# Where five modulation blocks and one feature transposition stand in two attention loops of a float32 two-block network

## The chip, the cores and the metric

The kernel runs on one core of a Trainium2 chip. The metric is the device time of one execution in microseconds (us); three runs of the kernel before gave 1543.00, 1543.26 and 1543.37 us, with a median of 1543.26 us.

## The reference, cut to what matters

The reference runs two networks one after the other over 256 tokens of width 1024, in float32. The change lies in layer 0 of the second network, in its mixer of two attentions. The input has 256 tokens of `x` and 256 tokens of `ctx`; a modulation vector, computed from `w_mod`, scales and shifts the normed input.

```python
mod_x = (s_x @ w_mod[l] + b_mod[l])[:, None, :]       # 6 x 1024 values, and the same for ctx
h_x = modulate(rms_norm(x, norm_g[l, 0]), sh1_x, sc1_x)
...
# even_mixer: grouped-query attention A (8 heads), then pairwise (differential) attention B (4 pairs)
o_a = map_query_blocks(lambda q: gqa_attend(q, ka_all, va_all), qa_x)
s = jnp.einsum('bqhjd,bshjd->bhjqs', q, k); p = softmax(s)          # B: two score maps per head pair
a = (p[:, :, 0] - lam * p[:, :, 1]); o_b = einsum('bhqs,bshe->bqhe', a, v)
o_b = (rms_norm(o_b, subln_g) * (1 - lam0))
out_x = jnp.concatenate([o_a, o_b], axis=-1) @ w_out
```

## The kernel before, in words

Every engine has its own instruction stream, written out by hand in the same order of work, and the streams meet at semaphores. `did(...)` raises the semaphore of an engine under a label, and `after(label)` is the value that another engine waits for. Float32 matrices are split into a high part (ScalarE, L1180) and a low part (VectorE, L1196), and each product is three matmuls (L601 to L603). All weights come in one stream of 1 MB chunks through SyncE's queue into three slots `raw` (L565). A chunk's DMA starts when the chunk three places before it in the stream has been used: a split weight chunk by VectorE's low part, a modulation chunk by TensorE itself, which reads it unsplit.

**PSUM banks.** TensorE takes a bank for each result with `job(label)`: the banks of a ring in turn, and it waits until the last result of that bank has been read. In both attentions of layer 0 the ring has seven banks, so that a job waits for the reader of the job seven places before it. The eighth bank, number 7, is taken by `side=2` alone. In the first attention it holds the two query blocks that `query_block` computes, in the second the first four products of the output projection (`product_block`).

**The first attention (`items_second(0, 0)`, kind A).** 32 items, each a head and a tile of 128 tokens: the first 16 with 256 keys, the others with 512. The loop `attend` runs over steps `i`. On TensorE a step does, in this order: the scores of items i and i+1, in even steps (L784); what `side_steps_halves` places there (turns of queries and keys, L1051; one eighth of a projection of queries, `query`, three matmuls); a modulation block if `mods_at` gives one; the transposes of the probabilities of item i-3 (L818); and the values of item i-4 (L846). A modulation block (`mod`, L732) is 16 matmuls over two raw chunks, and ahead of it come the four transposes of the modulation block before it (`turn_mod`, L716). ScalarE does per step: the copy of item i-3's transposed probabilities (L1369), the exponentials of item i (L1350), and then a turned query or key (L1617). VectorE does: the maxima of item i (L2032), the outputs of item i-5 (L2103). It copies a modulation row (L1945) in the step after TensorE's, ahead of the maxima in an even step and behind them in an odd one. Five blocks stand in this loop, in steps 3, 8, 13, 18 and 23. GpSimd computes the roots that scale queries and keys before they are turned (L2698, L2700).

**The second attention (kind B).** 16 items, each a head pair on a tile of 128 tokens: the first 8 with 256 keys, the others with 512. In step i TensorE does the two scores of item i (L784), side work, the transposes of item i-2 (L818) and the values of item i-3 (L846). The side work is two value projections (steps 1 and 3), the four turns `fo` of the mixed output into features (L687; steps 5, 6, 16 and 17), each read by ScalarE (L1244) and then by VectorE (L1811), and four products (steps 8 to 11). ScalarE: copy of item i-2's probabilities, two exponentials of item i, high part of a feature. VectorE: two maxima of item i (L2032), the combination of the two maps of item i-1 (L2077 to L2080), the outputs of item i-4 (L2098), and the low part of a feature, if one stands in the step.

The change touches `side_steps_pairs`, `side_steps_halves`, `mods_at`, `turn_feature` and `turn_mixed`.

Of the kernel before, what the change touches and what calls it, by code (L numbers as in the profile page):

```python
# [237 lines left out]
class Counts:  # L238
# [6 lines left out]
    def did(self, sem, *labels):  # L245

        n = self.now[sem] = self.now.get(sem, 0) + 1
        for label in labels:
            assert label not in self.marks, label
            self.marks[label] = (sem, n)  # L250
        return self.sems[sem], 1
# [8 lines left out]
    def after(self, *label):  # L260

        if self.known is None:
            return self.sems["tensor"], 1
        sem, n = self.known.marks[label]
        return self.sems[sem], n
# [15 lines left out]
def build(nc, T, out, counts):  # L281
    did, after = counts.did, counts.after
    with ExitStack() as ctx:
# [5 lines left out]
        def tile(stack, name, shape, dt=F32):  # L289
            return stack.enter_context(nc.sbuf_tensor(name, shape, dt))  # L290
# [73 lines left out]
        mix = tile(ctx, "mix", [P, 4, D])  # L364
# [113 lines left out]
        def side_steps_pairs():  # L478


            return ([(1, ("v2", 0, 1, 0)), (3, ("v2", 0, 1, 1))] + [(at, ("fo", j)) for j, at in enumerate((5, 6, 16, 17))]
                    + [(8 + k, ("product", k)) for k in range(4)]
                    + [(18 + n, ("weights", PLACE[UNIT["out2", 0, 1].w0] + n)) for n in range(2)])

# [16 lines left out]
        def side_steps_halves():  # L501

            return ([(0, ("keys", 0)), (1, ("keys", 1)), (4, ("roots",)),
                     (2, ("ahead", PLACE[UNIT["q2", 0, 1].w0] + 1)),
                     (9, ("turn", "q", 0)), (10, ("turn", "k", 0)), (11, ("turn", "q", 1)), (12, ("turn", "k", 1))]
                    + [(at, ("query", 2, k)) for k, at in enumerate((4, 5, 6, 7, 9, 10, 11, 12))]
                    + [(at, ("query", 3, k)) for k, at in enumerate((15, 16, 17, 19, 20, 21, 22, 24))]
                    + [(13, ("queries", 2)), (25, ("queries", 3))])

        def items_second(l, part):  # L510
# [8 lines left out]

        def mods_at(i, items, mods):  # L520

            n, beside = divmod(i - 3, 5)
            return [mods[n]] if beside == 0 and 0 <= n < len(mods) else []

        def item_info(it):

# [53 lines left out]
        def _(pe):  # L580
# [5 lines left out]
            def job(*label, side=0):  # L586

                banks = (state["banks"], (6, 7), (7,))[side]
                b = banks[turn[side] % len(banks)]
                turn[side] += 1  # L590
                if b in last:
                    pe.wait_ge(*after("read", *last[b]))
                last[b] = label
                counts.banks[label] = b
                return ps[:, b, :]
# [78 lines left out]
                    ins = mm(o[:, 0:rhs.shape[-1]], lhs, rhs, start=True, stop=True)  # L674
                ins.then_inc(*did("tensor", ("read", "spin", label)))

            def turn_feature(name, src, tiles, ready, j):

                o = job(name, j)
                if j == 0:  # L680
                    for r in ready:
                        pe.wait_ge(*after(*r))
                for q in range(2):
                    for i, t in enumerate(tiles):
                        k = 2 * j + q
                        c = (2 * q + i) * P
                        ins = nc.tensor.transpose(o[:, c:c + P], src(t)[:, k * P:k * P + P], ident[:, :])  # L687
                ins.then_inc(*did("tensor", (name, j)))

            def turn_features(name, src, tiles, ready):  # L690

                for j in range(4):
                    turn_feature(name, src, tiles, ready, j)

            def turn_mixed(l, g, j):

                tiles = (2 * g, 2 * g + 1)
                ready = []
                if j == 0:
                    ready = [("mixed out" if l else "first half out", l, t) for t in tiles]  # L700
                elif l == 0 and j == 2:
                    ready = [("mixed out", l, t) for t in tiles]
                for r in ready:
                    pe.wait_ge(*after(*r))
                turn_feature(("fo", l, g), lambda t: mix[:, t, :], tiles, [], j)

            pending = []

# [161 lines left out]
            def attend(items, mods, steps=()):  # L870

                lag = turned_behind(items)
                for i in range(len(items) + lag + 1):
# [38 lines left out]
                    for m in mods_at(i, items, mods):  # L912
                        mod(*m)
# [128 lines left out]
            for l in range(2):  # L1042
# [12 lines left out]
                for part in range(2 - l):  # L1055
# [32 lines left out]
                    beside = l == 1  # L1088
# [4 lines left out]
                    else:  # L1093
                        oldest = [state["banks"][(turn[0] + n) % 8] for n in range(8)]
                        state["banks"], turn[0] = [b for b in oldest if b != 7], 0
                    attend(items_second(l, part), mods_second(l, part),
                           side_steps_last() if beside else side_steps_pairs() if part else side_steps_halves())
                    if l == 0:
                        oldest = [state["banks"][(turn[0] + n) % 7] for n in range(7)]
# [3 lines left out]
                if l == 0:  # L1103
                    for n in range(2):
                        by_token(UNIT["out2", 0, n], ("out2", 0, n), (2, 3), feat=None if n else ("fo", 0, 1), last=False,
                                 half_made=() if n else (2,))
                        if n == 0:
                            for j in range(4):
                                turn_mixed(0, 0, j)
# [4 lines left out]
                    for g in (1, 0):  # L1114
                        for j in range(2):
                            for e in range(4):
                                if (g, j, e) == (1, 1, 2):
                                    turn_normed(0, 1, 0)
                                by_feature(UNIT["in", 0, j], ("in", 0, j, g), g * S, g * S + S, feat=None if j else ("n2", 0, g),
                                           tiles=[e], first=g == 1, last=g == 0)  # L1120
# [15 lines left out]
                for j in range(4):  # L1136
                    turn_mixed(1, 0, j)
# [83 lines left out]
        def _(act):  # L1221
# [381 lines left out]
            for l in range(2):  # L1603
# [41 lines left out]
                for part in range(2 - l):  # L1645
# [45 lines left out]
                    if l == 1:  # L1691
                        act.wait_ge(loads["odd"], 48)
                        save_gates(1)
                    attend(items, side_steps_last() if l else side_steps_pairs() if part else side_steps_halves())
                for t in range(nt):
                    act.wait_ge(*after("mixed out", l, t))
# [90 lines left out]
        def _(dve):  # L1787
# [341 lines left out]
            def attend(items, mods, steps=()):  # L2129
                for i in range(len(items) + 5):  # L2130
                    if i % 2 == 0:
                        for m in mods_at(i - 1, items, mods):
                            mod_row(*m)
                    if i < len(items):
                        maxima(i, items[i])
                    if i % 2:
                        for m in mods_at(i - 1, items, mods):
                            mod_row(*m)
# [307 lines left out]
            for l in range(2):  # L2446
# [33 lines left out]
                if l == 0:  # L2480
                    for key in (("q", 3), ("k", 2), ("k", 3)):
                        head_sums(*key)
                    head_roots(1)
                    for what in "qk":
                        for t in (2, 3):
                            head_scaled(what, t)
                    split_lo(PLACE[UNIT["q2", 0, 1].w0], st)
                    for t in (0, 1):
                        head_sums("q", t)
                    dve.wait_ge(loads["late"], 32)  # L2490
                    link(v.tensor_scalar(sublng[:, :], sublng[:, :], 1.0 - LAM0, None, ALU.mult))
                    items = items_second(0, 0)
                    attend(items, mods_second(0, 0), side_steps_halves())
# [10 lines left out]
                else:  # L2504
# [10 lines left out]
                    gate_rows(1)  # L2515
                items = items_second(l, 1 - l)
                attend(items, mods_second(l, 1 - l), side_steps_last() if l else side_steps_pairs())
                if l == 0:
                    split_to(("out2", 0, 1), 0)
# [263 lines left out]
```

## Time and profile before

| what | value |
|---|---|
| three runs | 1543.00, 1543.26, 1543.37 us |
| the profiled execution's own time | 1543.38 us |
| its span, first to last instruction | 1541.4 us |
| TensorE matmul busy | 1509.1 us, 98% of the span |
| VectorE busy | 905.8 us, 59% |
| ScalarE busy | 656.2 us, 43% |
| mean granted TensorE clock | 0.997 |

The profile is of one execution. An idle time in square brackets behind a row is the time in which the engine had nothing running before that instruction, with what ended the wait. Matmuls overlap in the engine, so the start of one row to the start of the next is the pace, and a row's own duration is longer. The first attention's loop runs from about 565 to 645 us, the second's from 693 to 745 us.

### The profile page before, as it was taken

The numbers are of one execution on the slowest core, as the hardware profiler recorded it, in microseconds if no ns is written. First come the engines' busy times: TensorE is split into PE (matmuls) and PEld (weight loads), VectorE is DVE, ScalarE is ACT, GpSimd is POOL, SyncE is SP. The second block draws the span as 40 slices with busy tenths as digits, with TensorE's granted clock in tenths as the row PEclk, the third lists the DMA queues.
The fourth block names the chain that finished last, engine by engine and source line by source line (L and its number), as shares of the span: only waits on it lengthen the run. The fifth ranks groups of instructions, "written<-read, shape, count | busy, mean of one in ns | idle before, by whom it ended". The sixth has DMA issues, their size and how long they took to land.

```text
span 1541.4 us, 22913 instructions
## 1 busy us (share of the span) xinstructions
PE 1509.1 (98%) x8906; PEld 1253.3 (81%) x8906; DVE 905.8 (59%) x1551; ACT 656.2 (43%) x1025; POOL 167.0 (11%) x179
## 2 busy tenths in 40 slices
PE   9999999999999998999999999999999999999998
PEld 7998798888897775786799777777787877878886
DVE  5785674756565883546775343334448645667655
ACT  5464334444443543535554222231224546654342
POOL 2200220000000110001223101111011030001010
PEclk9999999999999999999999999999999999999999
DMA  6456564453537325211232353544422421245451
GB/s 247 184 206 235 220 220 174 178 192 137 189 118 266 112 85 220 107 68 47 83 137 80 139 219 128 200 166 162 191 82 93 141 83 55 98 149 219 184 197 56
DMA packets 43764, 233.73 MB, mean 152 GB/s; under 512 B 13264, under 2 KB 14224, under 8 KB 16784
## 3 DMA queue, kind: packets, MB, share of 16 engines
q1 hardware_dynamic: 31232, 222.38, 39.0%
q10 hardware_dynamic: 12432, 9.94, 2.3%
q8 instruction: 72, 1.18, 0.3%
q14 instruction: 28, 0.23, 0.0%
HBM read 231.22 MB, written 1.08 MB: 151 GB/s over the span
## 4 chain that ended last, share of the span: by engine, by line
PE 85%; DVE 8%; ACT 2%; issue 1%; POOL 1%; DMA 1%; SPq 0%; DVEq 0%; ACTq 0%
PE ps L601 19%; PE ps L603 19%; PE ps L602 19%; PE ps L649 9%; PE ps L846 5%; PE ps L651 4%; PE ps L818 3%; PE ps L784 2%; DVE wlo L1196 2%; PE ps L732 2%; PE ps L776 2%; POOL f L2623 1%; DMA raw<-in_wstream 1%; ACT whi L1180 1%; PE ps L716 1%
## 5 line engine op out<-in xcount | busy, mean ns | idle before, releaser
L1196 DVE TENSOR_TENSOR wlo<-raw,whi 128x2048 fp32r<-128x2048 f32 x148 | 342.5, 2335 | 188.0 <-ACT whi L1180 187.7
L1180 ACT ACTIVATE whi<-raw 128x2048 fp32r<-128x2048 f32 x160 | 301.5, 1907 | 237.5 <-PE ps L603 161.5
L601 PE MATMUL ps<-whi,f 128*128 128x512 f32 (+1 forms) x608 | 215.3, 354 | 3.1 <-DVE f L1811 1.0
L603 PE MATMUL ps<-whi,f 128*128 128x512 f32 (+1 forms) x608 | 209.8, 345 | 0.0
L602 PE MATMUL ps<-wlo,f 128*128 128x512 f32 (+1 forms) x608 | 209.6, 345 | 0.0
L601 PE MATMUL ps<-f,whi 128*128 128x256 f32 (+1 forms) x640 | 206.8, 323 | 1.9 <-DVE wlo L1196 1.7
L603 PE MATMUL ps<-f,wlo 128*128 128x256 f32 (+1 forms) x640 | 205.0, 320 | 0.0
L602 PE MATMUL ps<-f,whi 128*128 128x256 f32 (+1 forms) x640 | 204.9, 320 | 0.0
L649 PE MATMUL ps<-f,whi 128*128 128x512 f32 x576 | 202.8, 400 | 1.9 <-DVE kq L2017 1.6
L601 PE MATMUL ps<-whi,hhi 128*128 128x512 f32 x384 | 152.7, 398 | 0.0
L603 PE MATMUL ps<-whi,hlo 128*128 128x512 f32 x384 | 151.8, 395 | 0.0
L602 PE MATMUL ps<-wlo,hhi 128*128 128x512 f32 x384 | 151.8, 395 | 0.0
L651 PE MATMUL ps<-f,wlo 128*128 128x256 f32 x504 | 141.4, 280 | 0.0
L601 PEld LDWEIGHTS ps<-f,whi 128*128 128x128 f32 x640 | 121.8, 190 | 20.5 <-issue 6.5
L601 PEld LDWEIGHTS ps<-whi,f 128*128 128x128 f32 x608 | 115.2, 189 | 28.1 <-issue 9.2
L603 PEld LDWEIGHTS ps<-f,wlo 128*128 128x128 f32 x640 | 121.8, 190 | 8.9
L602 PEld LDWEIGHTS ps<-f,whi 128*128 128x128 f32 x640 | 121.9, 190 | 8.5
L603 PEld LDWEIGHTS ps<-whi,f 128*128 128x128 f32 x608 | 115.1, 189 | 14.2
L649 PEld LDWEIGHTS ps<-f,whi 128*128 128x128 f32 x576 | 104.8, 188 | 26.3 <-issue 3.0
L602 PEld LDWEIGHTS ps<-wlo,f 128*128 128x128 f32 x608 | 115.3, 190 | 12.2
L2634 POOL TENSOR_TENSOR hlo<-htmp,hhi 128x256 fp32r<-128x256 f32 (+1 forms) x64 | 60.5, 946 | 423.9 <-ACT hhi L1547 423.9
L651 PEld LDWEIGHTS ps<-f,wlo 128*128 128x128 f32 x504 | 95.2, 189 | 2.5
(298 smaller groups left out, 2187.7 us busy)
## 6 DMA issues: line engine op xcount, KB each, us to landing
raw<-in_wstream SPq DMA_DIRECT2D x210, 1024.0 KB, 5.0
gates<-gated ACTq DMA_DIRECT2D x6, 512.0 KB, 4.3
hx<-in_x SPq DMA_DIRECT2D x1, 1024.0 KB, 5.4
lnrow<-in_ln_g ACTq DMA_DIRECT2D x2, 512.0 KB, 4.0
lnrow<-in_ln_b ACTq DMA_DIRECT2D x2, 512.0 KB, 5.4
hc<-in_ctx ACTq DMA_DIRECT2D x1, 1024.0 KB, 5.5
mix<-in_rpb_rows ACTq DMA_DIRECT2D x4, 256.0 KB, 4.6
hc<-in_rpb_rows ACTq DMA_DIRECT2D x4, 256.0 KB, 3.7
```

Source lines behind the costliest of these rows:

```text
L601: mm(o, lh, rh, start=start, stop=False)
L602: mm(o, lh, rl, start=False, stop=False)
L603: return mm(o, ll, rh, start=False, stop=stop)
L649: ins = mm(both, wh, parts_f[:, :, k, c0:c0 + S], start=k == 0, stop=k == KD - 1)
L651: mm(o[:, 0:S], wl, fhi[:, k, c0:c0 + S], start=False, stop=False)
L732: ins = mm(o[at:at + 32, :], condz[:, 2 * k:2 * k + 32], raw[:, c % RAW_SLOTS, base:base + NW], start=k < 4, stop=k >= 4, tile_position=(0 ...
L776: ins = mm(o, kq1[po:po + DH, l % 2, 1, j * 2 + tq, t * P:t * P + P], kq1[po:po + DH, l % 2, 0, j * 2 + tq, 0:n], start=True, stop=True)
L818: ins = nc.tensor.transpose(o[:, (j - b) * P:(j - b + 1) * P], e[:, j * P:j * P + P], ident[:, :])
L846: ins = mm(o[:, 0:dv], p[:, i % 2, j * P:j * P + P], v, start=j == 0, stop=j == kt - 1)
L1180: nc.scalar.activation(whi[:, w % SPLIT_SLOTS, :], raw[:, c % RAW_SLOTS, :], ACT.Copy, scale=QSCALE if SPLIT[w][0].name[0] == "q" else 1.0 ...
L1196: ins = nc.vector.tensor_tensor(low, raw[:, c % RAW_SLOTS, :], high, ALU.subtract)
L2634: p.tensor_tensor(hlo[:, j % 2, e, cols], htmp[:, e % 2, cols], hhi[:, j % 2, e, cols].bitcast(F32), ALU.subtract).then_inc(*did("pool", * ...
```

## The change

Three edits. First, the five modulation blocks of the first attention stand in steps 3, 9, 14, 19 and 24 in place of 3, 8, 13, 18 and 23; VectorE's copies of their rows follow by the same function, in steps 4, 10, 15, 20 and 25. Second, the eighths of the query projections that stood in the blocks' new steps take the steps that come free: the fifth eighth of token tile 2 goes from step 9 to 8, and for tile 3 the fourth from 19 to 18 and the last from 24 to 23. Third, in the second attention the first feature turn goes from step 5 to step 4 on TensorE, ScalarE and VectorE, and the first two turns (steps 4 and 6) are written to bank 7 and take no place in the ring of seven.

```diff
-            return ([...] + [(at, ("fo", j)) for j, at in enumerate((5, 6, 16, 17))]
+            return ([...] + [(at, ("fo", j)) for j, at in enumerate((4, 6, 16, 17))]
...
-                    + [(at, ("query", 2, k)) for k, at in enumerate((4, 5, 6, 7, 9, 10, 11, 12))]
-                    + [(at, ("query", 3, k)) for k, at in enumerate((15, 16, 17, 19, 20, 21, 22, 24))]
+                    + [(at, ("query", 2, k)) for k, at in enumerate((4, 5, 6, 7, 8, 10, 11, 12))]
+                    + [(at, ("query", 3, k)) for k, at in enumerate((15, 16, 17, 18, 20, 21, 22, 23))]
...
         def mods_at(i, items, mods):
-            n, beside = divmod(i - 3, 5)
-            return [mods[n]] if beside == 0 and 0 <= n < len(mods) else []
+            return [m for at, m in zip((3, 9, 14, 19, 24), mods) if at == i]
...
-            def turn_feature(name, src, tiles, ready, j):
-                o = job(name, j)
+            def turn_feature(name, src, tiles, ready, j, side=0):
+                o = job(name, j, side=side)
...
-                turn_feature(("fo", l, g), lambda t: mix[:, t, :], tiles, [], j)
+                turn_feature(("fo", l, g), lambda t: mix[:, t, :], tiles, [], j, side=2 if (l, g) == (0, 1) and j < 2 else 0)
```

## Rows read from the trace of the kernel before

**Rows 1.** The page, busy time of each engine.

```profile
PE 1509.1 (98%) x8906; PEld 1253.3 (81%) x8906; DVE 905.8 (59%) x1551; ACT 656.2 (43%) x1025; POOL 167.0 (11%) x179
```

**Rows 2.** Busy time by stretch: length, PE, PEld, DVE, ACT, POOL, clock, DMA.

```profile
577.00:640.00 63.00, 57.63 (x403) 39.71 (x402) 26.15 (x83) 29.24 (x81) 4.52 (x10) 1.00 0.45 175
...
640.00:700.00 60.00, 60.00 (x314) 50.32 (x312) 27.38 (x47) 22.49 (x33) 0.00 (x0) 1.00 0.29 106
...
710.00:745.00 35.00, 31.66 (x202) 21.90 (x201) 30.71 (x83) 27.06 (x90) 11.26 (x34) 1.00 0.00 1
```

**Rows 3.** TensorE's waits, 568 to 645 us: total, times, longest.

```profile
PE ps L784 <- ACT e L1350: 2.0, 3, 1.0
PE ps L846 <- ACT e L1350: 1.9, 2, 0.9
PE ps L732 <- DMA raw<-in_wstream: 1.5, 1, 1.5
```

**Rows 4.** TensorE's timeline, steps 8 and 9 of the first attention: start, length.

```profile
579.53 0.66 PE L716 MATMUL ps<-ident,modrow 128*128 128x128 f32 x4
580.12 1.07 PE L732 MATMUL ps<-raw,condz 128*32 128x512 f32 x8
582.68 1.06 PE L732 MATMUL ps<-raw,condz 128*32 128x512 f32 x8 [1.49 <-DMA raw<-in_wstream]
583.67 0.44 PE L818 MATMUL ps<-ident,e 128*128 128x128 f32 x2
...
585.49 0.38 PE L818 MATMUL ps<-ident,e 128*128 128x128 f32 x2
586.80 0.66 PE L846 MATMUL ps<-vv,p 128*128 128x64 f32 x4 [0.93 <-ACT e L1350]
```

**Rows 5.** The chain of waits, 574 to 583 us: start, length.

```profile
574.75 7.89 DMA raw<-in_wstream
```

**Rows 6.** GpSimd's timeline: the first scaling of queries.

```profile
578.82 1.04 POOL L2698 TENSOR_TENSOR mix<-mix,hrs 128x512 f32<-128x512 f32 x1
```

**Rows 7.** ScalarE's timeline, steps 9 and 12.

```profile
586.19 0.47 ACT L1350 ACTIVATE e<-ps,nmax 128x256 f32<-128x256 f32 x1
...
594.81 0.38 ACT L1617 ACTIVATE kT<-ps 128x256 f32<-128x256 f32 x1
```

**Rows 8.** TensorE's timeline, steps 12, 14 and 16.

```profile
593.67 0.38 PE L818 MATMUL ps<-ident,e 128*128 128x128 f32 x2
...
598.62 0.70 PE L784 MATMUL ps<-kT,qT 64*128 64x256 f32 x4
...
601.38 1.13 PE L784 MATMUL ps<-kT,qT 64*128 64x512 f32 x4
```

**Rows 9.** TensorE's timeline, steps 19 and 20.

```profile
610.21 0.60 PE L818 MATMUL ps<-ident,e 128*128 128x128 f32 x4
...
612.17 1.13 PE L784 MATMUL ps<-kT,qT 64*128 64x512 f32 x4 [0.96 <-ACT e L1350]
```

**Rows 10.** TensorE's timeline, second attention, steps 7 and 8.

```profile
716.20 0.70 PE L784 MATMUL ps<-kT,qT 64*128 64x256 f32 x4 [1.15 <-DVE mix L2098]
...
719.51 0.38 PE L818 MATMUL ps<-ident,e 128*128 128x128 f32 x2
```

**Rows 11.** ScalarE's timeline, second attention, step 5: the first feature.

```profile
712.96 0.60 ACT L1244 ACTIVATE f<-ps 128x512 fp32r<-128x512 f32 x1
```

**Rows 12.** VectorE's timeline, second attention, steps 4 to 7.

```profile
710.41 0.34 DVE L2098 TENSOR_SCALAR mix<-ps,rinv 128x128 f32<-128x128 f32 x1
...
713.60 0.69 DVE L1811 TENSOR_TENSOR f<-ps,f 128x512 fp32r<-128x512 f32 x1 [1.07 <-ACT f L1244]
...
716.53 0.69 DVE L1811 TENSOR_TENSOR f<-ps,f 128x512 fp32r<-128x512 f32 x1 [0.47 <-ACT f L1244]
717.13 0.75 DVE L2032 TENSOR_REDUCE nmax<-ps 128x1 f32<-128x256 f32 x2
...
718.64 0.35 DVE L2098 TENSOR_SCALAR mix<-ps,rinv 128x128 f32<-128x128 f32 x1
```

More of the change, by code:

```diff
@@ L478, in side_steps_pairs @@
         def side_steps_pairs():
-            return ([(1, ("v2", 0, 1, 0)), (3, ("v2", 0, 1, 1))] + [(at, ("fo", j)) for j, at in enumerate((5, 6, 16, 17))]
+            return ([(1, ("v2", 0, 1, 0)), (3, ("v2", 0, 1, 1))] + [(at, ("fo", j)) for j, at in enumerate((4, 6, 16, 17))]
                     + [(8 + k, ("product", k)) for k in range(4)]
```

## The prediction, made before the changed kernel had run

> **What bounds the kernel now.** I read the page's busy times first, then the busy time by stretch, then TensorE's waits in the two loops that the change touches, and last the timelines of the four engines around each wait. TensorE is busy for 98% of the span [rows 1], so an edit that adds and removes no TensorE work can only change its idle time. In the two loops that idle time is small. From 577 to 640 us it is 63.00 - 57.63 = 5.37 us, from 710 to 745 us it is 35.00 - 31.66 = 3.34 us, and between the loops nothing [rows 2]. So 8.7 us is all that could be won, 0.56% of the time. The 5.37 us are six waits: three of scores and two of values for a bank whose last content ScalarE's exponentials still read, 3.9 us together, and one of a modulation block for its second raw chunk, 1.49 us [rows 3, 4].
>
> The profiled execution took 1543.38 us around a span of 1541.4; the median of the runs shown is 0.12 us lower. All sums are made against 1543.38. A difference under 0.2%, 3.1 us, is what a measurement of this kernel can hardly tell from no change.
>
> **How one wait is priced.** The exponentials of item i stand on ScalarE behind the copy of the probabilities that TensorE transposes in the same step. A bank that waits for exponentials of the current step is therefore free only a fixed time after those transposes start: 586.80 - 585.49 = 1.31 us for 256 keys [rows 4], 612.17 - 610.21 = 1.96 us for 512 [rows 9]. The exponential itself frees the bank 586.80 - 586.19 = 0.61 us after its own start [rows 4, 7]. Whatever TensorE does in between shortens the idle time.
>
> **Edit 1, the second modulation block goes from step 8 to 9, and an eighth of a projection (three matmuls) from 9 to 8.** In the kernel before, the block starts at 580.12, its second half waits for the chunk and starts at 582.68, and the block is left at 583.67: 3.55 us for 16 matmuls [rows 4]. Without the wait eight take 0.99 us at that pace, so a whole block some 1.85. After the change, step 8 goes on at 579.53 with the eighth (0.78), two transposes (0.22) and a set of values (0.39), then step 9's turn of queries (0.37); my unit times are paces between starts in the same timeline. That is 581.29. The four transposes of the previous row take 580.12 - 579.53 = 0.59, the first half 0.93, and the second half is due at 582.81. The chunk's DMA was under way from 574.75 and had landed by 582.64 [rows 5]. What its start waited for is earlier than step 8 and does not move. So the wait goes, with 0.13 us to spare. Item 6's transposes start at 583.76 in place of 585.49: a gain of **1.73 us**. The turned queries need GpSimd's scaling, which starts at 578.82 and takes 1.04 us [rows 6]; 580.92 is late enough. VectorE's copy of the row now stands ahead of step 10's maxima, but the block has ended long before those scores exist. Costed at nothing; it would cost its 0.7 us if the scores were ready first.
> The 0.93 us wait that follows in step 9 depends on transposes and exponentials that keep their order. It stays, and so does the next one, in step 12.
>
> By the rows the transfer took 7.89 us, with another 1 MB ahead of it in flight. The Trainium skill, page DMA: Bandwidth & Descriptors, section "Anatomy of one DMA — SWDGE (gpsimd) path", gives about 2.0 us fixed plus the bytes at 436 GB/s (fitted for transfers that GpSimd issues). By that page two of them would be an estimated 6.8 us, the wait in the kernel before only 0.4 us and the gain 0.6; the row shows the longer wait, so the measurement decides.
>
> **Edit 2, the third block goes from step 13 to 14.** Step 13 now holds nothing but transposes and values. The jobs of the ring are the same in number, in another order. Counting back seven places: the values of item 9, which waited for exponentials 13 (0.93 us), now take a bank long free, but the scores of items 14 and 15 take banks of exponentials 12 and 13. Exponentials 13 stand behind the turned key copy at 594.81 [rows 7], 0.29 for it and 0.28 for the probability copy, so they start at 595.38 and free the bank at 595.99. In the old clock the scores then start there instead of at 598.62 [rows 8], and block and row transposes follow, so that item 11's transposes start at 595.99 + 0.63 + 0.58 + 1.86 = 599.06 against 599.26. A wait of 1.0 us has replaced one of 0.93. Then scores 16, which waited for nobody, take the bank of exponentials 15: item 12's transposes start at 599.06 + 0.27 + 0.39 + 0.78 = 600.50, plus 1.31 is 601.81 against 601.38 [rows 8]. **Loss 0.43 us** for edit 2 in all. ScalarE and VectorE have no further wait in between by the counts.
>
> **Edit 3, fourth and fifth block.** Step 18 gets an eighth, 19 the block; the wait of 0.96 us at scores 20 keeps its order and stays [rows 9]. At scores 24 the 0.52 us wait, one of the three, goes (they take banks of values 17 and exponentials 22). But values 21 now wait for exponentials 24, due 1.96 us after transposes 21 where 1.72 us of work stand, and scores 26 wait for exponentials 25: 0.24 + 0.36. Chaining the paces gives scores 26 at 629.47 against 629.48 in the old clock: **0**. The last block's chunks are freed 1.9 us later; SyncE's queue then loads the next weights, and TensorE has not one wait from 640 to 700 [rows 2], so there is cover.
> First attention: 1.73 - 0.43 + 0.00 = **1.30 us**.
>
> **Edit 4, the first feature turn goes one step earlier, both turns leave the ring.** TensorE's wait of 1.15 us ahead of scores 7 [rows 10] is for a bank whose output VectorE reads late; with two jobs fewer in the ring that bank is another, and scores 7 could start about 715.0 in place of 716.20. But who is behind is VectorE. In the kernel before it waits twice there, 1.07 + 0.47 us, for ScalarE's high part of a feature [rows 12], and from 713.60 on it hardly rests. After the change its low part of feature 0 stands in step 4, behind outputs 0 (710.41, paced to 710.75) and ahead of maxima 5. ScalarE's high part comes behind copy 2, which is 0.25 late because the turn stands ahead of its transposes, and two exponentials: I get 710.88 in place of 712.96 [rows 11], so VectorE waits 0.78. Item 5's maxima start 1.5 us later, which delays exponentials 5, combination 5 and transposes 4 (714.2 against 713.8). Feature 1's high part then comes at 715.83, and VectorE waits 0.65. Its waits sum to 1.43 against 1.54, and maxima 7 start at 717.02 against 717.13 [rows 12]. Item 6's transposes then need outputs 3 read, 718.64 - 717.13 + 0.27 + 0.13 = 1.91 us later: 718.93 at best, say 719.05, against 719.51 [rows 10]. TensorE could be there at 718.6, so it idles for the difference. **Gain 0.45 us**, of the 1.2 that the ring alone would give. After that the loop is TensorE's and the shift is kept.
> Bounds where the trace of before shows no such order: this edit +1.2 (VectorE follows) to -1.76 (below); edit 1 between 0 and 1.73; edits 2 and 3 together between -1.5 (two more waits of 0.5 to 1.0) and +0.9 (no new wait).
>
> Sum: 1.30 + 0.45 = 1.75; 1543.38 - 1.75 = 1541.6, against the median 1541.5.
>
> **The rivals.**
> 1. VectorE is no bound in the second loop, and the ring's 1.2 us is kept: 1543.26 - 1.30 - 1.2 = 1540.8. For it: TensorE has four waits within 6 us of that loop, and the longest [rows 10] is the one that the ring takes away. Against: VectorE is busy 30.71 of 35 us there [rows 2]. With edit 2's new waits smaller too, 1540.0.
> 2. Only the first loop gains; in the second, transposes 4, late by 0.4, are not made good: 1543.26 - 1.30 + 0.4 = 1542.4. For it: VectorE's order is strictly that of the program.
> 3. The change doesn't do what it says: the chunk lands as late relative to the block as before, or the time won waits at the next bank. 1543.26 + 0.43 - 0.45 = 1543.2. Against: the landing is fixed at 582.64 and the next wait counts from the transposes. For it: a margin of 0.13 us.
> 4. The other side. VectorE's low part of feature 0, now ahead of maxima 5, waits as long as it did (1.07 us) and its own 0.69 comes on top, and the second wait isn't shortened for it. Then exponentials 5, combination 5 and all that follows are 1.76 us late, and TensorE with them: 1543.26 - 1.30 + 1.76 = 1543.7, slower. It decides where maxima 7 start more than 1.3 us later, against the shift of the first loop, than in the kernel before. Against: ScalarE's two exponentials of item 4 are ready when the copy of item 2 is, 709.7.
>
> **How the numbers follow.** Forecast 0.52, its own range 1540.9 to 1542.2; rival 1 0.16, rival 2 0.17, rival 3 0.08, rival 4 0.07. The likeliest is 1541.5. The range 1539.9 to 1543.3 takes in rivals 1 to 3 and leaves out rival 4 and a gain above 3.4 us. None of the cases as worked out reaches 3.1 us; faster by over 0.2% needs rival 1 with edits 2 and 3 at their upper bound: 0.07. Slower by over 0.2% needs rival 4 with edits 2 and 3 at their lower bound: 0.03. The same: 0.90.
>
> **What would show it.** The modulation block of step 9 as 16 matmuls in one row without a wait for the DMA; item 6's transposes 1.7 us earlier; a wait of about 1.0 us ahead of scores 14 and one of 0.6 ahead of scores 16, none at scores 24; in the second loop maxima 7 no later than before against the first loop's shift, no wait at scores 7, one at transposes 6. TensorE's idle time should be near 4.7 us in the first loop. It is wrong if the wait for the DMA is still there, if the waits for exponentials sum to over 5 us, or if the trace after 745 us has new idle time.

## The result and the profile after: slower, by a wait in layer 1

| kernel | median | runs | lowest to highest |
|---|---|---|---|
| before | 1542.95 us | 14 | 1541.32 to 1543.52 |
| changed | 1546.33 us | 14 | 1545.73 to 1547.33 |

The ratio of all runs is 1.0025, 95% interval 1.0018 to 1.0032, which is 3.9 us; the medians differ by 3.4 us. The changed kernel is slower. Forecast were 1541.5 us, a range that ended at 1543.3, and a chance of 0.03 for slower by over 3.1 us. The profiled executions say the same: 1546.13 us after (span 1544.0), 1543.38 before (span 1541.4).

The page hides the loss. First the busy times of the changed kernel, beside [rows 1]: TensorE is busier by 1.4 us with as many matmuls, so some of them ran longer. VectorE is busier by 2.2 us, which lies in its low parts (L1196: 2357 ns each in the mean, 2335 before); e5_copy_early below has the same 2357 ns and no loss, so that isn't the cause.

```profile
PE 1510.5 (98%) x8906; PEld 1253.6 (81%) x8906; DVE 908.0 (59%) x1551; ACT 656.4 (43%) x1025; POOL 167.0 (11%) x179
```

Next the stretches of [rows 2] in the changed kernel: length, then PE, PEld, DVE, ACT and POOL busy with counts, granted clock, DMA share, GB/s.

```profile
577.00:640.00 63.00, 58.76 (x413) 40.90 (x411) 26.45 (x84) 30.32 (x84) 4.31 (x9) 1.00 0.45 173
...
710.00:745.00 35.00, 32.17 (x201) 22.27 (x200) 30.85 (x83) 27.77 (x89) 12.47 (x40) 1.00 0.01 1
...
1200.00:1220.00 20.00, 16.17 (x110) 13.73 (x109) 11.82 (x30) 11.08 (x21) 0.00 (x0) 0.91 0.53 179
```

Both loops have less idle time at TensorE than before: 4.24 us where 5.37 stood, and 2.83 where 3.34 stood. The stretch that lost is one that the prediction never looked at, the start of the second layer's pairwise attention. The same stretch in the kernel before:

```profile
1200.00:1220.00 20.00, 18.52 (x141) 15.93 (x139) 14.60 (x41) 13.03 (x26) 0.00 (x0) 1.00 0.54 181
```

The changed kernel, although it comes to this stretch earlier, runs 31 matmuls fewer in it, and the mean granted clock is 0.91 in place of 1.00. TensorE's timeline of the changed kernel there follows (start, length, operation, idle time before with what ended it). Line numbers move by up to three between kernels: the products at L601 to L603 before are L600 to L602 here.

```profile
1204.30 0.27 PE L742 MATMUL ps<-ident,gcol 128*32 128x128 f32 x1
1205.20 1.13 PE L784 MATMUL ps<-kT_b,qT_b 64*128 64x512 f32 x4 [0.62 <-ACT kT_b L1617]
1209.25 0.58 PE L600 MATMUL ps<-f,whi 128*128 128x256 f32 x1 [2.93 <-DVE grow L2192]
1209.63 0.42 PE L601 MATMUL ps<-f,whi 128*128 128x256 f32 x1
1209.85 0.42 PE L602 MATMUL ps<-f,wlo 128*128 128x256 f32 x1
...
1212.51 0.28 PE L600 MATMUL ps<-f,whi 128*128 128x256 f32 x1
...
1216.55 1.13 PE L784 MATMUL ps<-kT_b,qT_b 64*128 64x512 f32 x4
```

And of the kernel before:

```profile
1206.06 0.27 PE L742 MATMUL ps<-ident,gcol 128*32 128x128 f32 x1
1206.95 1.13 PE L784 MATMUL ps<-kT_b,qT_b 64*128 64x512 f32 x4 [0.62 <-ACT kT_b L1617]
1208.01 0.39 PE L601 MATMUL ps<-f,whi 128*128 128x256 f32 x1
...
1213.96 1.13 PE L784 MATMUL ps<-kT_b,qT_b 64*128 64x512 f32 x4
```

At the transpose of layer 1's gate row (L742) the changed kernel is 1.76 us ahead. That this is nearly the 1.75 of the forecast is chance: 0.27 of it is an earlier start of this execution, and the two loops give 0.95 and 0.52. From there to the second pair of scores it takes 12.25 us and the old kernel 7.90: 4.35 us lost in one place. VectorE's timeline of the changed kernel shows who is behind:

```profile
1204.02 2.29 DVE L1196 TENSOR_TENSOR wlo<-raw,whi 128x2048 fp32r<-128x2048 f32 x1
1206.72 2.29 DVE L1196 TENSOR_TENSOR wlo<-raw,whi 128x2048 fp32r<-128x2048 f32 x1 [0.40 <-ACT whi L1180]
1208.93 0.27 DVE L2192 COPY grow<-ps 32x128 f32<-32x128 f32 x1
```

The gate row's copy stands behind two splits of weight chunks, 2.29 us each, in both kernels. In the old one nobody waited for it: counted from the code, the gate row lay in bank 2 of the ring, whose next user (transposed probabilities of layer 1's first item) comes behind two projections. In layer 1 the ring is cut to banks 0 to 5, and banks 6 and 7 are used for projections beside the attention (`side=1` in `job`). Edit 4 (the feature turns; edits are numbered as in the prediction) took two jobs out of the ring of seven, so that the jobs after it take other banks: the gate row now lies in bank 6. The first projection beside the attention writes to bank 6, and has to wait for that copy.

### The profile page after: what moved, and what is told of

It is laid out like the page before. It is cut to its first block, busy times and chain, and to the rows that moved or that the text cites. A ratio compares the mean times of both kernels' runs of the same rounds, so it can differ in the third digit from the quotient of the medians.

```text
span 1544.0 us, 22913 instructions
## 1 busy us (share of the span) xinstructions
PE 1510.5 (98%) x8906; PEld 1253.6 (81%) x8906; DVE 908.0 (59%) x1551; ACT 656.4 (43%) x1025; POOL 167.0 (11%) x179
## 4 chain that ended last, share of the span: by engine, by line
PE 86%; DVE 8%; ACT 3%; issue 1%; POOL 1%; DVEq 0%; ACTq 0%
PE ps L600 19%; PE ps L602 19%; PE ps L601 19%; PE ps L648 9%; PE ps L846 5%; PE ps L650 4%; PE ps L818 3%; PE ps L732 3%; DVE wlo L1196 2%; PE ps L784 2%; PE ps L776 2%; POOL f L2623 1%; ACT whi L1180 1%; ACT f L1244 1%; PE ps L716 1%
## 5 line engine op out<-in xcount | busy, mean ns | idle before, releaser
L1196 DVE TENSOR_TENSOR wlo<-raw,whi 128x2048 fp32r<-128x2048 f32 x148 | 345.8, 2357 | 186.8 <-ACT whi L1180 186.4
L600 PE MATMUL ps<-whi,f 128*128 128x512 f32 (+1 forms) x608 | 215.3, 354 | 3.1 <-DVE f L1811 1.0
L600 PE MATMUL ps<-f,whi 128*128 128x256 f32 (+1 forms) x640 | 207.5, 324 | 4.3 <-DVE grow L2192 2.9
L602 PE MATMUL ps<-whi,f 128*128 128x512 f32 (+1 forms) x608 | 209.9, 345 | 0.0
L601 PE MATMUL ps<-wlo,f 128*128 128x512 f32 (+1 forms) x608 | 209.6, 345 | 0.0
L601 PE MATMUL ps<-f,whi 128*128 128x256 f32 (+1 forms) x640 | 205.6, 321 | 0.0
L602 PE MATMUL ps<-f,wlo 128*128 128x256 f32 (+1 forms) x640 | 205.5, 321 | 0.0
L600 PE MATMUL ps<-whi,hhi 128*128 128x512 f32 x384 | 152.7, 398 | 0.0
L602 PE MATMUL ps<-whi,hlo 128*128 128x512 f32 x384 | 151.9, 395 | 0.0
L601 PE MATMUL ps<-wlo,hhi 128*128 128x512 f32 x384 | 151.8, 395 | 0.0
L600 PEld LDWEIGHTS ps<-f,whi 128*128 128x128 f32 x640 | 122.5, 191 | 22.9 <-issue 5.8
L600 PEld LDWEIGHTS ps<-whi,f 128*128 128x128 f32 x608 | 115.1, 189 | 28.5 <-issue 9.6
L602 PEld LDWEIGHTS ps<-f,wlo 128*128 128x128 f32 x640 | 122.5, 191 | 8.9
L601 PEld LDWEIGHTS ps<-f,whi 128*128 128x128 f32 x640 | 122.6, 192 | 8.5
L602 PEld LDWEIGHTS ps<-whi,f 128*128 128x128 f32 x608 | 115.1, 189 | 14.2
L601 PEld LDWEIGHTS ps<-wlo,f 128*128 128x128 f32 x608 | 115.3, 190 | 12.3
```

The costliest lines, as they stand in the source:

```text
L600: mm(o, lh, rh, start=start, stop=False)
L601: mm(o, lh, rl, start=False, stop=False)
L602: return mm(o, ll, rh, start=False, stop=stop)
L1196: ins = nc.vector.tensor_tensor(low, raw[:, c % RAW_SLOTS, :], high, ALU.subtract)
```

## The experiments

Three segments of TensorE's timeline carry all of the comparison. A is the first attention's loop (first modulation block to the first turn after the loop), B the second attention's (from its gate row to its last values), and S the stretch above, from layer 1's gate row to the second pair of scores. What lies between them takes the same time in every kernel within 0.1 us, but for e3_before_row6, whose gate row comes 0.3 us later. The segments are those of the one profiled execution, in us. The ratio, from 6 to 14 runs of each kernel, is to the kernel before on the same chip, with its 95% interval; it uses all runs and isn't the quotient of the medians.

| kernel | median us | ratio | A | B | S |
|---|---|---|---|---|---|
| before | 1542.95 | | 75.99 | 49.98 | 7.90 |
| changed | 1546.33 | 1.0025 [1.0018, 1.0032] | 75.04 | 49.46 | 12.25 |
| e1_blocks | 1542.25 | 0.9998 [0.9989, 1.0007] | 75.02 | 49.97 | 7.89 |
| e2_features | 1546.78 | 1.0026 [1.0016, 1.0036] | 76.02 | 49.47 | 13.11 |
| e3_before_row6 | 1547.03 | 1.0030 [1.0019, 1.0041] | 74.84 | 49.98 | 12.08 |
| e4_after_skip | 1541.89 | 0.9995 [0.9986, 1.0004] | 75.06 | 49.46 | 7.89 |
| e5_copy_early | 1541.79 | 0.9997 [0.9988, 1.0006] | 75.05 | 49.46 | 8.20 |
| e6_place | 1541.94 | 1.0000 [0.9991, 1.0009] | 75.02 | 49.66 | 7.90 |
| e7_step_only | 1541.90 | 0.9995 [0.9986, 1.0004] | 74.52 | 49.99 | 8.05 |
| e8_best | 1541.17 | 0.9992 [0.9983, 1.0001] | 74.35 | 49.46 | 7.89 |
| e9_spin | 1546.92 | 1.0031 [1.0018, 1.0043] | 75.02 | 49.46 | 13.05 |
| e10_spin3 | 1544.79 | 1.0013 [1.0004, 1.0022] | 75.04 | 49.46 | 10.90 |
| e11_bank_only | 1542.39 | 0.9998 [0.9989, 1.0007] | 76.00 | 49.72 | 7.89 |
| e12_before_again | 1543.03 | 1.0001 [0.9992, 1.0010] | 75.77 | 49.98 | 8.06 |

The medians from e1 on were taken on three chips, on which that of the kernel before was 1542.97 (e1 to e4), 1542.28 (e5, e6, e8, e9) and 1542.75 us (e7, e10, e11, e12), so only ratios and segments compare one experiment with another. Counted from the code, layer 1's gate row lies in bank 2 in before, e1, e6, e7 and e12, in bank 6 in changed, e2, e3, e5, e9 and e10, and in bank 1 in e4, e8 and e11.

**e1_blocks: before with edits 1 to 3 (blocks and query eighths) alone.**

```diff
+            return [m for at, m in zip((3, 9, 14, 19, 24), mods) if at == i]
+  query 2: (4, 5, 6, 7, 8, 10, 11, 12)   query 3: (15, 16, 17, 18, 20, 21, 22, 23)
```

> The kernel before with edits 1 to 3 alone: blocks in steps 3, 9, 14, 19, 24, the query eighths moved; the feature turns as before. Theory (T): the prediction's terms hold and the loss comes from edit 4 alone, by the bank in which layer 1's gate row lies. Then this kernel is 1.3 us faster than the kernel before (ratio 0.9992), and its trace has no wait for the gate row's copy (L2192) and a granted clock of 1.00 from 1200 to 1220 us. Rival (R): the later release of the last blocks' chunks, or the new order, costs time somewhere later; then it is slower than before by 1 us or more.

No loss: S is as before, and A has the whole of the first loop's gain. By its runs the kernel isn't clearly faster (0.9998, where 0.9992 was expected); the account of edit 1 below says why.

**e2_features: before with edit 4 alone.**

```diff
+  fo: (4, 6, 16, 17)
+  turn_feature(..., j, side=2 if (l, g) == (0, 1) and j < 2 else 0)
```

> The kernel before with edit 4 alone: first feature turn in step 4, the first two in bank 7, out of the ring. T: 0.5 us gained in the second attention, then the gate row of layer 1 falls on bank 6, TensorE waits 2.9 us for its copy and runs the next dozen matmuls at a lower clock, 1.3 us: +3.7 us (ratio 1.0024). R: the loss belongs to the edits together or to the first loop: within 1 us of the kernel before.

The loss comes with edit 4 alone. S is 0.86 us longer than in the changed kernel with the same wait of 2.93 us, since here 23 matmuls run slowly behind it and not 14. TensorE's waits of this kernel in 1100 to 1300 us (total, times, longest) begin with

```profile
PE ps L601 <- DVE grow L2193: 2.9, 1, 2.9
```

**e3_before_row6: before, with places of the ring passed over until the gate row falls in bank 6.** Nothing else differs.

```diff
             def gate_rows(l):
+                while l and state["banks"][turn[0] % len(state["banks"])] != 6:
+                    turn[0] += 1
                 o = job("grow", l)
```

> The kernel before, unchanged but for layer 1's gate row: the ring is moved on until its next bank is 6 (4 places), so that the row lies in the bank that the first side projection takes. T: this alone costs 2.9 us of waiting and 1.3 us of lower clock: +4.2 us (ratio 1.0027), with the same row of a wait for L2192. R (the bank is not the cause, something else made VectorE's copy late or TensorE slow there): within 0.5 us of before.

The loss appears in the old kernel without any edit (the ring passes over six places by the code, not four): S is 12.08 and the same stretch has the same wait and a low clock.

```profile
PE ps L601 <- DVE grow L2194: 2.9, 1, 2.9
```

```profile
1200.00:1225.00 25.00, 20.75 (x142) 17.51 (x140) 13.87 (x40) 14.56 (x26) 0.00 (x0) 0.93 0.47 153
```

**e4_after_skip: the changed kernel, with banks 6 and 7 passed over for the gate row.**

```diff
+                while l and state["banks"][turn[0] % len(state["banks"])] > 5:
+                    turn[0] += 1
```

> The changed kernel, but layer 1's gate row takes the ring's next bank that is not 6 or 7. T: the wait and the lower clock go, the gains of both loops stay: 1.75 us faster than the kernel before (ratio 0.9989), 4.2 us faster than the changed one. R: no faster than before, since the gains of the loops are lost at a later wait.

The gains of both loops stay in A and B; the ratio, 0.9995, shows less than the 0.9989 expected, and its interval takes in both 1 and that. The wait goes, S is 7.89, and this stretch is full again (compare e3's row above):

```profile
1200.00:1225.00 25.00, 23.50 (x175) 20.05 (x175) 17.73 (x50) 16.95 (x33) 0.00 (x0) 1.00 0.58 180
```

**e5_copy_early: the changed kernel, gate row still in bank 6, its copy ahead of the second split on VectorE.**

```diff
-                    split_lo(ahead + 2, st)
+                    split_lo(ahead + 1, st)
                     gate_rows(1)
+                    split_lo(ahead + 2, st)
```

> The changed kernel, the gate row still in bank 6, but VectorE copies it (L2192) ahead of the last of its two weight chunks (2.3 us, and 0.4 us of wait for it) and not behind them. T: the wait at the first side projection shrinks from 2.9 to about 0.4 us, the clock stays at 1.00, and the kernel is 1.3 us faster than the kernel before (ratio 0.9991). R (the bank, by itself, is slow to write, whoever reads it): it stays at +3.4 us.

The bank alone doesn't cost the time: it needs the late copy too. In this kernel VectorE's copy starts at 1206.35 between the splits, S is 8.20, and TensorE's wait is

```profile
PE ps L600 <- DVE grow L2192: 0.2, 1, 0.2
```

**e6_place: the changed kernel, with a ring place passed over for each turn in bank 7.**

```diff
             def turn_feature(name, src, tiles, ready, j, side=0):
+                if side:
+                    turn[0] += 1
```

> The changed kernel, where each of the first two feature turns goes to bank 7 and the ring passes over the place that it would have taken, so that all later jobs have the banks of the kernel before. T: the gate row is back in bank 2, no wait for L2192, clock 1.00. In the second attention the jobs behind the turns wait for the same readers as in the kernel before, and the 0.5 us gained there may go or shrink: 1.3 to 1.8 us faster than the kernel before (ratio 0.9990). R: the second attention loses more than 1 us with it, VectorE's order (feature 0 ahead of the maxima) now being felt.

With the old phase kept the gate row is in bank 2 and S is 7.90. B is 49.66 and not 49.46: 0.2 us of the second loop's gain came from the ring's new phase. The ratio is 1.0000, where 0.9990 was expected.

**e9_spin and e10_spin3: how much of the 4.35 us is the clock.** The changed kernel with idle-filling matmuls of 512 columns, which compute nothing that is used, at the place of the wait: six (e9), three (e10). The profile lists each of them as two.

```diff
+                        if i == 0 and items[0][0] == "C":
+                            spin("hold", modrow[:, 0:P], modrow[:, :], 6)
```

> The changed kernel, with six extra matmuls 128x512 of no use, written to the ring's next bank, between the first two scores of layer 1 and the first side projection, so that TensorE is busy for most of the 2.9 us in which it waited. T: the wait is no shorter in sum, but the clock stays at 1.00 and the slower matmuls behind it go: 1.3 us faster than the changed kernel, 2 us slower than before (ratio 1.0014). R (the lower clock has nothing to do with the idle time): as slow as the changed kernel (1.0025).

> As the kernel with extra matmuls between the first scores of layer 1 and the first side projection, but three of them: the six took 4.8 us, more than the 2.9 us of waiting, and three should take 2.4. T: the wait and the extra matmuls together are no longer than the wait was, the matmuls behind run at full pace, and the kernel is 1.1 us faster than the changed one (ratio to before 1.0017). R: the lower clock comes back, ratio 1.0025.

Six took 4.85 us, longer than the wait, and the kernel gained nothing (1.0031, where 1.0014 was expected): the projection started only at 1211.10. But the clock stayed at 1.00 and the projection took 6.24 us where it had taken 1216.55 - 1209.25 = 7.30. Three fit:

```profile
1206.32 2.84 PE L673 MATMUL ps<-modrow 128*128 128x512 f32 x6
1209.32 0.39 PE L600 MATMUL ps<-f,whi 128*128 128x256 f32 x1 [0.15 <-DVE grow L2194]
1209.54 0.28 PE L601 MATMUL ps<-f,whi 128*128 128x256 f32 x1
```

```profile
1200.00:1220.00 20.00, 18.93 (x127) 14.77 (x127) 11.88 (x30) 11.51 (x22) 0.00 (x0) 1.00 0.52 179
```

The first fence is TensorE's timeline, the second the busy time by stretch. The projection starts no earlier than in the changed kernel, yet S falls to 10.90. So the wait itself costs 10.90 - 7.90 = 3.0 us and the lower clock after it 12.25 - 10.90 = 1.35 us. The second part isn't fixed. Behind the same wait of 2.93 us the lower clock costs 13.11 - 10.90 = 2.2 us in e2, and in e3 1.5 us (from the first to the second pair of scores, 11.49 against 10.01).

**e7_step_only (before, first turn in step 4, in the ring) and e11_bank_only (before, both turns in bank 7 at the old steps, banks 6 and 7 passed over for the gate row): edit 4 split.**

```diff
+  e7:  fo: (4, 6, 16, 17), no side
+  e11: fo: (5, 6, 16, 17), side=2 for j < 2, and the two lines of e4
```

> The kernel before with only the first feature turn in step 4 and not 5, both turns in the ring as before. T: the gate row stays in bank 2, so no wait for L2192; the second attention, which is VectorE's in these steps, is 0.2 to 0.5 us shorter than its 49.98 us, since VectorE waits 0.1 us less and the turn fills TensorE's time: ratio 0.9997. R: the gain of the second attention belongs to the bank alone: 49.98 us or longer.

> The kernel before with the first two feature turns in bank 7 but at their old steps 5 and 6, and the gate row moved off banks 6 and 7. T: the second turn must wait in bank 7 until VectorE has read the first, which it does one step later than in the changed kernel, so the gain of 0.5 us in the second attention goes or turns: between 49.9 and 50.6 us for it, ratio 1.0000 to 1.0004. R: the bank alone makes the gain: 49.5 us, ratio 0.9997.

The earlier step alone gives nothing in B (49.99, where 0.2 to 0.5 less was expected), the bank alone 0.26 (49.72, between what T and R named), both together 0.52. TensorE's waits in the second loop (690 to 745 us), first of e7, then of e11:

```profile
PE ps L687 <- DVE mix L2098: 1.0, 1, 1.0
PE ps L784 <- DVE mix L2098: 0.6, 1, 0.6
```

```profile
PE ps L687 <- DVE f L1814: 1.5, 1, 1.5
PE ps L821 <- DVE mix L2101: 0.9, 2, 0.6
```

Either half alone moves a wait to the second feature turn (L687): in e7 it waits for the output that its ring bank still holds, in e11 for VectorE to read the first turn out of bank 7. e7's ratio of 0.9995 says nothing of the edit: its interval takes in 1, and in its profiled execution the first loop had no wait for the DMA.

**e8_best: what the other runs point to.** Edit 1 and edit 4 without edits 2 and 3 (blocks in steps 3, 9, 13, 18, 23, the third tile's query eighths as before), and the gate row kept out of banks 6 and 7.

```diff
+            return [m for at, m in zip((3, 9, 13, 18, 23), mods) if at == i]
```

> The version that the terms point to: only the second block moved (steps 3, 9, 13, 18, 23; the fifth eighth of tile 2 in step 8, tile 3's eighths as before), the feature turns as changed, the gate row in the ring's next bank that is not 6 or 7. T: 1.73 us from the DMA wait without the 0.43 us that the third block cost, and 0.5 us in the second attention: 2.2 us faster than the kernel before (ratio 0.9986), 0.4 us faster than the changed kernel with the gate row moved. R: the third block's move paid for itself in a way the terms miss, and this is no faster than that kernel.

A is 74.35, 0.69 less than in the changed kernel with edits 2 and 3. It has the lowest ratio of all (0.9992, where 0.9986 was expected), and its median is 1.1 us under that of the kernel before on its chip, but the interval just reaches 1.

**e12_before_again: an exact copy of the kernel before.**

> The kernel before once more, to see how much one program differs from itself. T: the wait of the second modulation block for its chunk differs between executions (1.49 and 0.35 us in two profiles of this order), so the first attention takes 76.0 or 74.9 us and edit 1 is worth 1.7 or 0.6 us; the ratio is 1.000 within 0.001. R: the wait is 1.5 us again and the 0.35 was special to that kernel.

The ratio is 1.0001, and the half-width of its interval, 0.0009, is 1.4 us, less than half of the 3.1 us that the prediction took for hardly distinct from no change. The wait for the chunk is 1.27 us here.

## Why the prediction was wrong

The step that failed is the last sentence on edit 4: "After that the loop is TensorE's and the shift is kept." It was worked out for the two loops and put at no cost, without a reason, for the 800 us behind them. I had followed the ring as a distance, how many jobs back a bank's last user stands. That is enough while all eight banks are alike, and it isn't where a later part takes banks by number. Taking two jobs out of the ring changes the number of the bank for the jobs behind them, up to the place where banks 6 and 7 are set aside. What stood there in the place of "kept": 4.35 us lost, shown by e3 (the loss without the change), e4 and e6 (the change without the loss), e5 (it needs the copy behind the splits) and e2 (edit 4 alone). No rival named it. The one that ended slower put the loss on VectorE in the second loop, where none was. Only the last sign of being wrong applied: the trace after 745 us has new idle time.

The other terms, one by one:

**Edit 1, forecast +1.73.** In the changed kernel's timeline the block runs in one piece:

```profile
579.25 0.50 PE L600 MATMUL ps<-whi,f 128*128 128x512 f32 x1
...
581.11 0.60 PE L716 MATMUL ps<-ident,modrow 128*128 128x128 f32 x4
581.64 1.92 PE L732 MATMUL ps<-raw,condz 128*32 128x512 f32 x16
583.49 0.44 PE L818 MATMUL ps<-ident,e 128*128 128x128 f32 x2
...
584.86 0.66 PE L846 MATMUL ps<-vv,p 128*128 128x64 f32 x4 [0.93 <-ACT e L1350]
...
594.12 0.70 PE L784 MATMUL ps<-kT,qT 64*128 64x256 f32 x4 [0.83 <-ACT e L1350]
...
598.61 0.38 PE L818 MATMUL ps<-ident,e 128*128 128x128 f32 x2
...
600.12 1.13 PE L784 MATMUL ps<-kT,qT 64*128 64x512 f32 x4 [0.73 <-ACT e L1350]
...
610.93 1.13 PE L784 MATMUL ps<-kT,qT 64*128 64x512 f32 x4 [0.96 <-ACT e L1350]
```

The forecast had step 8 go on at 579.53 with the eighth, here it does so at 579.25: this execution is 0.28 us earlier before the edit begins. Item 6's transposes start at 583.49, and 583.76 - 0.28 = 583.48 was the forecast. In this pair of executions the step's mechanism is right to 0.01 us, and the next wait is 0.93, unchanged as said. (The margin of 0.13 us in the forecast counts from the second half's old start at 582.68; from the landing it is 582.81 - 582.64 = 0.17.) But the size of the gain isn't fixed. In the six profiles with the block in step 8 (before, e2, e11, e12, e3, e7) the wait for the chunk was 1.49, 1.50, 1.5, 1.3, 0.35 and 0 us: the landing is not "fixed at 582.64". The forecast priced one execution. Where the chunk is in time, edits 1 to 3 lose: A is 74.52 in e7, against 75.04 in the changed kernel and 74.35 in e8_best, so that edit 1 is worth 0.17 us there and all three together -0.52.

The Trainium skill's page DMA: Bandwidth & Descriptors, section "Anatomy of one DMA — SWDGE (gpsimd) path", gives the figure from which the prediction had an estimated wait of 0.4 us for two such transfers. One of the six executions (e3, 0.35 us) agrees with that estimate, four fit the row.

The times of the runs fit two kinds of execution: of all 102 runs of the kernel before, 34 lie from 1541.2 to 1542.0 us, 64 from 1542.4 to 1544.1, and 4 between. The copy, e12_before_again, has 4 of its 11 runs up to 1542.0 and 7 from 1543.0 on. The profiled executions lie on the side that fits: e7, without the wait, took 1541.75 us, before, e11 and e12, with it, 1543.38 to 1543.55. e1_blocks, where the block no longer waits, has all 11 from 1541.95 to 1542.69, and e8_best all 11 from 1540.6 to 1541.6. That the two groups are the executions with and without the wait is argued, not shown.

**Edit 2, forecast -0.43.** The two new waits are there, 0.83 ahead of scores 14 and 0.73 ahead of scores 16, where 1.0 and 0.6 were named. Scores 16 stood at 601.38 [rows 8]; less 0.28 and the 1.73 that is 599.37, and they start at 600.12: a loss of 0.75. Of the 0.32 that it was off, 0.12 had built up by item 12's transposes (598.61 where 600.50 - 0.28 - 1.73 was forecast), and 0.20 lie in the price of the wait: scores 16 start 1.51 us after these transposes, not 1.31. e8_best against e4_after_skip gives the same in A, 0.69 to 0.71 for edits 2 and 3. A mis-sized term, right in sign.

**Edit 3, forecast 0.** Scores 20 are at 610.93, which is 612.17 [rows 9] less 0.28 and 0.96; A as a whole is 0.95 shorter. So edit 3 is worth 0 within 0.02, and the wait of 0.96 is kept. Its inner terms hold too: there is no wait at scores 24, values 21 start 0.68 us behind the transposes ahead of them (626.97 and 626.29) where the pace in this loop is 0.44, and scores 26 start 1.28 us after values 21 where it is 0.94. That is 0.24 and 0.34 us of waiting, against 0.24 and 0.36 forecast. First attention: 0.95 where 1.30 was forecast.

**Edit 4 in its own loop, forecast +0.45.** Measured 49.98 - 49.46 = 0.52. VectorE's timeline of the changed kernel shows the forecast's argument at work:

```profile
709.18 0.35 DVE L2098 TENSOR_SCALAR mix<-ps,rinv 128x128 f32<-128x128 f32 x1
710.27 0.69 DVE L1811 TENSOR_TENSOR f<-ps,f 128x512 fp32r<-128x512 f32 x1 [0.75 <-ACT f L1244]
...
715.15 0.69 DVE L1811 TENSOR_TENSOR f<-ps,f 128x512 fp32r<-128x512 f32 x1 [0.64 <-ACT f L1244]
715.76 0.74 DVE L2032 TENSOR_REDUCE nmax<-ps 128x1 f32<-128x256 f32 x2
```

Its two waits sum to 1.39 (forecast 1.43, [rows 12] 1.54). Outputs 0 to maxima 7 take 6.58 us, where they took 717.13 - 710.41 = 6.72. On TensorE the wait of 1.15 at scores 7 is gone, and waits ahead of transposes took its place:

```profile
712.88 0.41 PE L818 MATMUL ps<-ident,e 128*128 128x128 f32 x2 [1.14 <-DVE mix L2098]
...
714.65 0.41 PE L818 MATMUL ps<-ident,e 128*128 128x128 f32 x2 [0.28 <-DVE mix L2098]
...
717.75 0.41 PE L818 MATMUL ps<-ident,e 128*128 128x128 f32 x2 [0.29 <-DVE mix L2098]
```

The last, at transposes 6, is the one that was named: forecast was 719.05 in the old clock, which less the loop's earlier start (693.22 - 692.00 = 1.22) is 717.83. The reason for the gain was less well understood than its size: I had expected the earlier step alone to bring some of it, and it brings none (e7).

The sum of the loops is 0.95 + 0.52 = 1.47 us for 1.75 forecast. Without the wait in layer 1 (e4_after_skip) the kernel is at 1541.89 us, 1.1 below the median of the kernel before on its chip (0.8 by the ratio); by its interval that is not distinct from no change. With it, 1.47 - 4.35 = -2.9 for the two profiled executions, which differ by 2.75. That all runs together differ by 3.4 to 3.9 fits a gain of edit 1 that is small in some executions and a clock loss that can exceed 1.35 us, but neither share is measured.

## What to carry to other kernels

When a change adds or removes a turn of a rotating pool of buffers, follow the number of the buffer, not only the distance, to every later place that takes buffers by number or cuts the pool to a part, and ask there who reads late; a small read behind long work in an engine's order is what makes such a collision dear. Before a wait for a transfer is priced, look for it in more than one execution. To an idle stretch of TensorE of some microseconds belongs what a lower clock can cost afterwards, here 1.35 to 2.2 us on top of 2.93.

## What the hardware showed that I had not expected

The clock. After the 2.93 us without a matmul the granted clock of the stretch is 0.91, and 14 matmuls of 128x256 run at a pace of 0.21 us (all but the first and last 0.41 or 0.42 long) before the rest return to 0.12 (0.28 long), a ratio of 1.8 (the engine's two levels are 1.2 and 2.4 GHz). With the idle time filled the clock is 1.00 and all but the first start 0.12 apart. The waits of up to 1.5 us in the two loops left it at 1.00 in every stretch read.

Between these lies a case that goes either way. All fourteen kernels are alike up to the place at 178 us where TensorE waits 2.08 or 2.09 us. In four of the profiles (before, e4, e7, e12) the clock falls behind that wait, to 0.68 to 0.80 in 180 to 185 us, and the transposes there take 2.59 to 3.50 us; in the other ten it stays at 1.00 and they take 1.94. The kernel before, then the changed one:

```profile
178.37 3.47 PE L687 MATMUL ps<-ident,hx 128*128 128x128 f32 x16 [2.09 <-DVE hx L1988]
```

```profile
178.47 1.94 PE L686 MATMUL ps<-ident,hx 128*128 128x128 f32 x16 [2.08 <-DVE hx L1988]
```

The length of an idle stretch alone does not fix what the clock does behind it.

The chunk. The same transfer, in kernels that are alike up to that place, was in time in one profile (e7) and 1.5 us late in three others; two profiles of one program, before and e12, gave 1.49 and 1.27. The first loop starts up to 0.8 us earlier or later (569.2 to 570.0). That limits what single profiles can say of changes this small: where no wait for a transfer and no fall of the clock stood in them, segments between landmarks agreed within 0.2 us.
